# Token rows first and unmodulated transposes in the prologue of a hybrid diffusion step

## The reference, cut to what matters

```python
mod = silu(c) @ ada_w + ada_b            # 6 rows of 1024 per group: sh1, sc1, g1, sh2, sc2, g2
h   = rms_norm(x, norm_mix_pre) * (1.0 + sc1) + sh1
proj = h @ w_in                          # 1024 x 3072: xl, yl, q, k, v, g
# then: gated linear recurrence, retention, w_out, router, 16 SwiGLU experts
```

## Time and profile before

| what | value |
|---|---|
| profiled execution, its own time | 1585.94 us |
| its span | 1583.7 us |
| PE busy | 1395.2 us (88%) |
| DVE busy | 681.2 us (43%) |
| ACT busy | 269.6 us (17%) |
| POOL busy | 126.9 us (8%) |
| HBM read | 464.59 MB, 302 GB/s over the span |
| first projection matmul | 62.33 us from the span's start |

### The profile page before, as it was taken

How to read it: one execution, slowest core, us unless ns; L and a number is a source line. 1 busy time by engine, 2 the same in 40 slices (tenths; PEclk the granted TensorE clock), 3 DMA queues, 4 the chain that set the end, 5 groups by cost and what they waited for, 6 DMA issues and landing times.

```text
span 1583.7 us, 26100 instructions
## 1 busy us (share of the span) xinstructions
PE 1395.2 (88%) x11009; PEld 616.5 (39%) x11009; DVE 681.2 (43%) x1219; ACT 269.6 (17%) x448; POOL 126.9 (8%) x81
## 2 busy tenths in 40 slices
PE   5799889777963899999999999999999999999990
PEld 1587666544850222233333333333333333333330
DVE  1535654341454435245343444443534435335343
ACT  2324444220330011101101111011110111101102
POOL 0422331120000000000000000000000000000000
PEclk9999999887976899999999999999999999999995
DMA  9421120357043999999999999999999999999973
GB/s 361 139 80 54 53 67 30 117 181 263 28 186 133 377 395 396 398 415 396 411 398 397 412 388 408 398 395 406 396 397 406 391 392 395 399 414 394 412 296 141
DMA packets 124272, 479.79 MB, mean 303 GB/s; under 512 B 11534, under 2 KB 13834, under 8 KB 107788
## 3 DMA queue, kind: packets, MB, share of 16 engines
q1 hardware_dynamic: 113796, 453.55, 72.9%
q0 software_dynamic: 3072, 10.49, 2.8%
q10 hardware_dynamic: 7304, 14.23, 2.5%
HBM read 464.59 MB, written 13.64 MB: 302 GB/s over the span
## 4 chain that ended last, share of the span: by engine, by line
PE 64%; DMA 22%; DVE 9%; ACT 3%; issue 2%; ACTq 0%; POOL 0%; SPq 0%; POOLq 0%; DVEq 0%
PE bank L1031 18%; DMA arena<-in_exp_up 13%; PE bank L1048 12%; PE bank L1036 9%; PE bank L1053 6%; DMA raw<-in_exp_up 5%; PE bank L359 3%; PE bank L360 3%; PE bank L361 3%; DMA raw<-in_ada_w 2%; PE bank L742 1%; DVE arena L1231 1%; PE bank L792 1%; PE bank L874 1%; PE bank L851 1%
## 5 line engine op out<-in xcount | busy, mean ns | idle before, releaser
L1031 PE MATMUL bank<-raw,xs_t 128*32 128x512 f32 x1056 | 257.3, 604 | 45.4 <-DMA raw<-in_exp_up 16.9
L1033 PE MATMUL bank<-raw,xs_t 128*32 128x512 f32 x1040 | 250.0, 602 | 0.0
L1031 PE MATMUL bank<-arena,xs_t 128*32 128x512 f32 x992 | 238.4, 596 | 6.2 <-DVE arena L1470 5.2
L1033 PE MATMUL bank<-arena,xs_t 128*32 128x512 f32 x1008 | 240.7, 599 | 0.0
L1467 DVE SCALAR_TENSOR_TENSOR arena<-bank,gate,arena 64x512 f32<-64x512 f32 x64 | 73.6, 1150 | 325.2 <-ACT arena L684 323.8
L1036 PE MATMUL bank<-raw,xs_t 128*16 128x512 f32 x1048 | 206.0, 603 | 0.0
L1036 PE MATMUL bank<-arena,xs_t 128*16 128x512 f32 x1000 | 198.0, 595 | 0.0
L1419 DVE STREAM_TRANSPOSE arena<-arena 32x256 f32<-32x256 f32 x372 | 161.8, 435 | 79.0 <-PE bank L1053 73.2
L684 ACT ACTIVATE arena<-bank 64x512 f32<-64x512 f32 x64 | 37.7, 588 | 831.1 <-PE bank L1036 830.3
L1031 PEld LDWEIGHTS bank<-raw,xs_t 128*32 128x32 f32 x1056 | 70.8, 111 | 207.7 <-issue 194.0
L1419 DVE STREAM_TRANSPOSE xs_t<-arena 32x256 f32<-32x256 f32 x204 | 88.8, 435 | 104.5 <-DMA arena<-xn_rows,slot_tok 101.5
(11 more groups left out here) (219 smaller groups left out, 1609.8 us busy)
## 6 DMA issues: line engine op xcount, KB each, us to landing
raw<-in_exp_gate SPq DMA_DIRECT2D x66, 1024.0 KB, 13.5
raw<-in_exp_up SPq DMA_DIRECT2D x65, 1024.0 KB, 14.5
arena<-in_exp_down SPq DMA_DIRECT2D x64, 1024.0 KB, 14.6
raw<-in_exp_down SPq DMA_DIRECT2D x64, 1024.0 KB, 12.6
arena<-in_exp_up SPq DMA_DIRECT2D x63, 1024.0 KB, 14.6
arena<-in_exp_gate SPq DMA_DIRECT2D x62, 1024.0 KB, 12.7
raw<-in_ada_w SPq DMA_DIRECT2D x24, 1024.0 KB, 9.1
raw<-in_w_in SPq DMA_DIRECT2D x12, 1024.0 KB, 5.9
```

What stands on the lines that cost most here:

```text
L1031: mm(psum[b][32 * i:32 * i + 32, :], lat[i], g[:, j, c], start=first, stop=final)
L1033: mm(psum[b][64 + 32 * i:96 + 32 * i, :], lat[i], u[:, j, c], start=first, stop=final)
```

## The change

- SP's queue issues the five loads of `x_in` ahead of all weights; ScalarE's queue no longer does. ScalarE's loads of the router weights and the rope tables come after the scaling of the token rows.
- ScalarE scales tiles 1 and 3, VectorE 0, 2 and 4.
- The second and third ada blocks change places (first half of the scale ahead of second half of the shift), and w0 lands ahead of a4.
- TensorE transposes the unmodulated rows between the first ada chunks; ScalarE (latent) and VectorE (context) bring them out into eight buffers `xT`. VectorE makes `hT_tmp` (now four buffers) from `xT` in SBUF. `hT_lo` is made by VectorE for k-tiles 0, 2, 4, 6, 7 and by GpSimd for 1, 3, 5.
- Chunk w0 goes k-tile by k-tile over all five output tiles, with the third ada block behind k-tile 0, the fourth ada block and the third's columns behind k-tile 1, and the fourth's columns behind k-tile 2. Then TensorE waits for k-tiles 4 to 7.

The core of the diff:

```diff
-ADA_FIRST = [0, 1, 2, 3]
+ADA_FIRST = [0, 2, 1, 3]
-LANDING = ([("a", i) for i in range(8)] + [("w", i) for i in range(12)] + ...
+LANDING = ([("a", i) for i in range(4)] + [("w", 0)] + [("a", i) for i in range(4, 8)] + [("w", i) for i in range(1, 12)] + ...
+    xT = [region(10240 + kt * TOK if kt < 4 else 2688 + (kt - 4) * TOK, TOK) for kt in range(KT)]
 # SP
+        for t in range(TILES):
+            sync.dma_start(x_in[:, t, :], x_lat[t * P:(t + 1) * P, :] if t < 4 else x_ctx).then_inc(x_ld[t], 16)
 # ScalarE
+            act.wait_ge(x_ld[t], 16)
...
+            nc.scalar.activation(junk0, x_in[:, t, :], ACT.Square, accum_out=...).then_inc(x_sq, 1)
+            if t == 2:
+                act.wait_ge(par_rd, 1)
+                nc.scalar.activation(sil, par[:, R_C:R_C + 16], ACT.Silu).then_inc(sil_rd, 1)
...
+        root(S_RSTD)
+        act.wait_ge(root_out, 1)
+        for t in (1, 3):
+            nc.scalar.mul(x_in[:, t, :], x_in[:, t, :], sm[:, S_RSTD + t:S_RSTD + t + 1]).then_inc(xn_act, 1)
         act.dma_start(rw[:, :, :], router_w.rearrange("(k p) n -> p k n", p=P)).then_inc(rw_in, 16)
         act.dma_start(rope_c, rope[0]).then_inc(rope_in, 16)
         act.dma_start(rope_s, rope[1]).then_inc(rope_in, 16)
+        for kt in range(KT):
+            xT_out(kt)
+            if kt == 5:
+                split_hi(act, 0)
+        for kt in range(4):
+            h_out(kt)
...
+        split_hi(act, 1)
+        for kt in range(4, KT):
+            h_out(kt)
+        split_hi(act, 2)
 # TensorE
+        pe.wait_ge(cond_rd, 1)
+        ada_block(0, 5)
+        pe.wait_ge(xn_rd, 3)
+        pe.wait_ge(xn_act, 2)
+        for kt in range(4):
+            turn_x(kt)
+        ada_half(1, 6, 0)
+        turn_x(4)
+        turn_x(5)
+        columns(0, 7, 128)
+        ada_half(1, 6, 1)
+        turn_x(6)
+        turn_x(7)
+        columns(1, 4, 128)
...
+            if n == 0:
+                for k in range(4):
+                    h_ready(pe, k)
+                    for u in range(TILES):
...
+                    if k == 0:
+                        pe.wait_ge(ada_row, 1)
+                        ada_block(2, 5)
+                    if k == 1:
+                        pe.wait_ge(ada_row, 2)
+                        ada_block(3, 6)
+                        pe.wait_ge(col_rd, 1)
+                        columns(2, 7, 128)
+                    if k == 2:
+                        pe.wait_ge(col_rd, 3)
+                        columns(3, 7, 128)
+                for kt in range(4, KT):
+                    h_ready(pe, kt)
+                continue
 # VectorE
+        row_copy(0, 5, rows[:, 0:512])
+        for kt in range(6):
+            xT_out(kt)
+        col_out(0, 7, 128)
         row_copy(1, 6, rows[:, 0:512])
+        xT_out(6)
+        xT_out(7)
         col_out(1, 4, 128)
+        aff_half(0)
+        h_out(0)
+        h_out(1)
+        split_lo(dve, "dve", 0)
+        h_lo_out(0)
+        h_out(2)
+        h_out(3)
+        h_lo_out(2)
+        row_copy(2, 5, rows[:, 0:512])
+        col_out(2, 7, 128)
         row_copy(3, 6, rows[:, 0:512])
+        col_out(3, 7, 128)
+        aff_half(1)
+        for kt in range(4, KT):
+            h_out(kt)
+            if kt >= 5:
+                if kt - 1 in (4, 6):
+                    h_lo_out(kt - 1)
+        split_lo(dve, "dve", 1)
+        h_lo_out(7)
+        split_lo(dve, "dve", 2)
 # GpSimd
+        split_lo(pool, "pool", 0)
+        h_lo_out(1)
+        h_lo_out(3)
+        split_lo(pool, "pool", 1)
+        h_lo_out(5)
+        split_lo(pool, "pool", 2)
```

More of the change, by code:

```diff
@@ L334, in expert_used, with h_ready @@
         eng.wait_ge(x_used, e * PER_E + (n - N_EXP + 1))
+    def h_ready(eng, kt):
+        if kt in (1, 3, 5):
+            eng.wait_ge(h_lop, kt // 2 + 1)
+        else:
+            eng.wait_ge(h_lo, {0: 1, 2: 2, 4: 3, 6: 4, 7: 5}[kt])
     def ret_sums(h):
@@ L453, in _, with xT_out, h_out @@
         root(S_RSTD)
[L454 to L455 removed]
+        act.wait_ge(root_out, 1)
+        for t in (1, 3):
+            nc.scalar.mul(x_in[:, t, :], x_in[:, t, :], sm[:, S_RSTD + t:S_RSTD + t + 1]).then_inc(xn_act, 1)
+        act.dma_start(rw[:, :, :], router_w.rearrange("(k p) n -> p k n", p=P)).then_inc(rw_in, 16)
+        act.dma_start(rope_c, rope[0]).then_inc(rope_in, 16)
+        act.dma_start(rope_s, rope[1]).then_inc(rope_in, 16)
+        def xT_out(kt):
+            act.wait_ge(xT_ps, kt + 1)
+            nc.scalar.copy(xT[kt][:, 0:LAT], psum[kt % 2][:, :]).then_inc(xe_lat, 1)
+        def h_out(kt):
+            act.wait_ge(h_tmp, kt + 1)
+            nc.scalar.copy(hT_hi[:, kt, :], hT_tmp[:, kt % 4, :]).then_inc(h_hi, 1)
+        for kt in range(KT):
[4 more added lines that the diff above has]
+            h_out(kt)
         act.wait_ge(lam_abs, 1)
         nc.scalar.activation(sm[:, S_EXP:S_EXP + 8], sm[:, S_ABS:S_ABS + 8], ACT.Exp, scale=-1.0).then_inc(lam_exp, 1)
[L459 to L461 removed]
+        split_hi(act, 1)
+        for kt in range(4, KT):
+            h_out(kt)
+        split_hi(act, 2)
         def yl_out(ct):
@@ L756, in columns, with turn_x @@
             last.then_inc(col_ps, 1)
[L759 to L773, removed]
+        def turn_x(kt):
             if kt >= 2:
-                pe.wait_ge(h_tmp, kt - 1)
+                pe.wait_ge(xe_lat, kt - 1)
+                pe.wait_ge(xe_ctx, kt - 1)
             for t in range(4):
@@ L820, in _ @@
             chunk_ready(pe, n)
-            pe.wait_ge(h_lo, 4 * (half + 1) if bi == 0 else KT)
             wh, wl = chunk_view(w_hi, n, 512), chunk_view(w_lo, n, 512)
+            if n == 0:
[3 more added lines that the diff above has]
+                        if k == 0:
+                            bank_free(0, u)
+                        if u < 4:
+                            last = three(psum[u][:, :], wh[:, k, u * P:(u + 1) * P], wl[:, k, u * P:(u + 1) * P],
+                                         hT_hi[:, k, 0:LAT], hT_lo[:, k, 0:LAT], k == 0, False)
+                        else:
+                            last = three(psum[4][:, :], hT_hi[:, k, LAT:], hT_lo[:, k, LAT:], wh[:, k, :], wl[:, k, :], k == 0, False)
+                    if k == 3:
+                        last.then_inc(w_used, 1)
+                    if k == 0:
+                        pe.wait_ge(ada_row, 1)
[11 more added lines that the diff above has]
+                continue
             for u in range(TILES):
@@ L1148, in _ @@
[L1148 to L1161, removed]
+        for t in (0, 2, 4):
+            ts(x_in[:, t, :], x_in[:, t, :], sm[:, S_RSTD + t:S_RSTD + t + 1], None, ALU.mult).then_inc(xn_rd, 1)
@@ new lines, in xT_out, with h_out @@
+        def xT_out(kt):
+            dve.wait_ge(xT_ps, kt + 1)
+            cp(xT[kt][:, LAT:], psum[2 + kt % 2][:, 0:P]).then_inc(xe_ctx, 1)
+        def h_out(kt):
+            if kt >= 4:
+                h_ready(dve, kt - 4)
+            else:
+                dve.wait_ge(xe_lat, kt + 1)
+                dve.wait_ge(xe_ctx, kt + 1)
+            ts(hT_tmp[:, kt % 4, 0:LAT], xT[kt][:, 0:LAT], aff[:, 0, 0, kt:kt + 1], modc[:, 0, kt:kt + 1], ALU.mult, ALU.add)
+            ts(hT_tmp[:, kt % 4, LAT:], xT[kt][:, LAT:], aff[:, 0, 1, kt:kt + 1],
+               modc[:, 1, kt:kt + 1], ALU.mult, ALU.add).then_inc(h_tmp, 1)
@@ new lines, in h_lo_out, with aff_half @@
+        def h_lo_out(kt):
+            dve.wait_ge(h_hi, kt + 1)
+            tt(hT_lo[:, kt, :], hT_tmp[:, kt % 4, :], hT_hi[:, kt, :], ALU.subtract).then_inc(h_lo, 1)
+        def aff_half(half):
+            k4 = slice(4 * half, 4 * half + 4)
+            dve.wait_ge(col_rd, 2 * half + 2)
+            for g in range(2):
+                step(stt(aff[:, 0, g, k4], modc[:, g, 8 + 4 * half:12 + 4 * half], 1.0, par[:, R_PRE + 4 * half:R_PRE + 4 * half + 4],
+                         ALU.add, ALU.mult))
@@ L1513, in _, with h_lo_out @@
         nc.gpsimd.memset(cond[:, :, :], 0.0).then_inc(cond_0, 1)
-        for n in range(WS):
-            split_lo(pool, "pool", n)
         nc.gpsimd.memset(gw[0], 0.0).then_inc(gw_0, 1)
+        def h_lo_out(kt):
+            pool.wait_ge(h_hi, kt + 1)
+            nc.gpsimd.tensor_tensor(hT_lo[:, kt, :], hT_tmp[:, kt % 4, :], hT_hi[:, kt, :], ALU.subtract).then_inc(h_lop, 1)
+        split_lo(pool, "pool", 0)
[4 more added lines that the diff above has]
+        split_lo(pool, "pool", 2)
         pool.wait_ge(col_ps, 4)
         nc.gpsimd.memset(gw[1], 0.0).then_inc(gw_0, 1)
-        for kt in range(KT):
-            pool.wait_ge(h_hi, kt + 1)
-            nc.gpsimd.tensor_tensor(hT_lo[:, kt, :], hT_tmp[:, kt % 2, :], hT_hi[:, kt, :], ALU.subtract).then_inc(h_lo, 1)
         for m in range(N_WOUT):
```

38 lines of the change are left out of this document (19 added, 19 removed).

## The result

The change made the kernel 1.0% faster, more than twice what I had forecast.

A forecast was written before the change was run, and what follows sets the result against it. Experts fill TensorE, busy 88%, untouched; the chain of waits in the first 66 us was asked. Its terms end w1 at 83.5 instead of 91.3, 7.8 us: 1585.94 - 7.8 = 1578.1, range 1573.3 to 1584.0.

The forecast's parts named there:

- Landings and token rows: Prologue loads and row scaling: a1 lands at 16.3 us, w0 at 26.2; rows are scaled by 16.9 and cost nothing.
- rival with the stuck queue: ScalarE stuck issuing rope loads until 23.2 us, time 1581.4; 20% together with one fall of the clock.
- TensorE to the end of the transposes: From 18.2 us, transposes, ada chunks and columns all at the low clock level, ending at 34.4.
- the clock never holds: TensorE stays at the low level to the last columns, costing 12.9 us; time 1591.0, slower; chance 5%.
- larger gain: VectorE ahead of w0 and w1: no blocking and `hT_tmp` at 0.6, 4.6 us more gained, time 1573.5; chance 10%.
- the blocking: GpSimd's subtraction holds up VectorE's SBUF operations, charged 1.54 us before the first matmul and again ahead of w1.
- VectorE to the first matmul: After the transposes, column step, `hT_tmp`, low split, GpSimd's 1.54 and `hT_lo`: TensorE starts w0 at 40.8 us.
- w0, k-tile by k-tile: TensorE from w0's start to the last columns: k-tile 0 5.2 us, the rest at the high level, together 17.7.
- The new wait: VectorE's work behind the last columns takes 9.7 us, to 68.2; TensorE idles 6.3 us behind k-tile 3.
- w1: Second projection chunk costs 13.5 + 1.8 us, its clock low after the idle time, ending at 83.5 instead of 91.3.
- The shift is carried: Everything behind w1 is written relative to TensorE, so the 7.8 us shift reaches the end unchanged.

The follow-up runs named there:

- filled front: Changed kernel with four extra matmuls on constants, results not used, ahead of the first ada block; 1570.28 us, 0.9899 to the kernel before.
- transposes in twos: Changed kernel with transposed k-tiles reordered: two, half an ada block, two, columns, half an ada block, four; 1571.31 us in one run.
- before, filled: Kernel before the change with TensorE's gaps between transposed k-tiles filled by matmuls whose results are not used; 1582.86 us, 0.9991 to the kernel before.
- x first: Kernel before the change with only the five x loads moved to the head of SP's queue; 1585.7 us, 0.9993 to the kernel before.
- tile order: Changed kernel with chunk w0 done tile by tile, all eight hT k-tiles and all modulation work ahead of it; 1567.23 us, 0.9867 to the kernel before.
- ada behind k-tile 0: Changed kernel with third and fourth ada blocks and both sets of columns right behind w0's first k-tile; 1566.39 us, 0.9861 to the kernel before.

## Why the prediction was wrong

I had the owners and the order of the waits right. The step that failed is the second: I priced TensorE's work up to the end of the transposes at the low level throughout. In the order of the prediction's steps:

1. **Landings and token rows: held.** Chunk a1 was used at 16.06 (said: 16.3), w0 rounded at 25.09 (said: 26.2), the extra table load is there at 9.22, 1.28 us. The rope loads took 0.60 and 0.80 us of ScalarE's queue, not 4.58: the rival with the stuck queue fell.
2. **TensorE to the end of the transposes: the step that failed.** I summed it all at the low level, 34.4; it was 28.39. The two stretches of after, TensorE alone, columns as above:

```profile
16.00:22.00 6.00, 5.94 (x27) 1.00 1.09 367
22.00:28.00 6.00, 6.00 (x53) 1.00 1.08 370
```

   Both show 6 us of unbroken work and a granted clock of 1.00, but the first holds 27 records and the second 53. The column reads 1.00 in the first too, where the durations are those of half speed; the durations, not the column, tell the level there. I took the low level from the kernel before, where ada work, columns and transposes ran slowly from 29 to 43 us, and did not bound the term from the other side, which the same operations later in the kernel offered. At the high level throughout the 16.2 us from 18.2 on are 8.1, so the bound would have been 26.3, and 28.39 lies inside. I looked at the clock only as a danger (the rival "the clock never holds"), not as a gain. Of my rivals the "larger gain" comes nearest in time, 1573.5, but by luck: it wanted no blocking, and the blocking is there (steps 3 and 5).
3. **VectorE to the first matmul: 4.75 instead of 6.4.** A k-tile of `hT_tmp` took 0.72, not 0.85, and GpSimd's price fell on GpSimd: its subtraction took 2.97 us (1544 ns mean in the earlier trace rows), since VectorE's split, begun at 30.45, was already under way at 31.37. VectorE's own `hT_lo` at 32.12 went ahead of it at its usual 0.81.
4. **w0, k-tile by k-tile: 19.0 instead of 17.7.** The clock fell in the gap of 4.75 us and stayed down for all of k-tile 0: 6.4 us for 15 matmuls (PEclk 0.53) where I had 5.2. How long it stays down is not the gap's length alone: behind 5.70 us in the filled front it was nine matmuls. From k-tile 1 on it ran high, as forecast: 12.7 us.
5. **The new wait: right, its size partly by luck.** 52.2 to 61.75 is 9.55 us, forecast 9.7; the idle time 5.9, forecast 6.3. The k-tiles (0.72 each) and the blocking (1.3) came out 0.8 us cheaper together, and handovers between the engines, which I had put at nothing, took about as much. VectorE's line in that place, timeline of after:

```profile
53.65 0.54 DVE L1212 TENSOR_SCALAR arena<-arena,aff,modc 128x512 f32<-128x512 f32 x1
...
55.27 1.83 DVE L1212 TENSOR_SCALAR arena<-arena,aff,modc 128x512 f32<-128x512 f32 x1
55.28 1.54 POOL L1610 TENSOR_TENSOR act_lo<-arena,act_hi 128x640 fp32r<-128x640 f32 x1 [6.08 <-ACT act_hi L476]
```

   The same scaling takes 0.54 us alone and 1.83 where GpSimd's subtraction, 1.54, starts within 0.01 us of it: 1.3 us more. The Trainium skill (SBUF — State Buffer, "Who interferes with whom") says of such a pair that whoever issues first has the shared ports for the whole instruction and the other is fully blocked. The trace agrees that one of the two waits, here VectorE, by 1.3 of the 1.54 us; which was issued first, starts 0.01 us apart don't tell. In step 3, where VectorE's operation is a subtraction with two inputs in SBUF, GpSimd pays.
6. **w1: 15.9 instead of 15.3**, low again behind the gap (PEclk 0.85).

The terms by size, steps 2 to 6: -6.0, -1.65, +1.3, -0.15, +0.6; together -5.9, and w1 ends at 77.6 where I had 83.5. Carried to the end, that makes 1572.2. The median is 1569.3. The terms are not independent: of 2.2 us taken from the transposes in the filled front, 1.2 reached the first projection matmul.

7. **The shift is carried: right to within 3 us.** Median less gates is 1461.2 for after and 1464.4 for before (1460.9 and 1461.7 the second time). These last 3 us are not settled. The interval of the gain, 13.6 to 18.7, includes the 13.7 us found up to gates, and the stretch behind gates differs by 5 us between two executions of the kernel before.

Open as well is what decides when the clock rises. The run of transposes is not it (transposes in twos), nor is any transpose needed. Timeline of TensorE in the kernel before and then in "before, filled", whose order up to 40 us is the same:

```profile
36.41 1.87 PE L754 MATMUL bank<-const,rows 128*128 128x2 f32 x8
```

```profile
32.48 3.52 PE L742 MATMUL bank<-raw,cond 128*32 128x512 f32 x16
35.92 1.05 PE L754 MATMUL bank<-const,rows 128*128 128x2 f32 x8
```

The same set of columns takes 1.87 us in one and 1.05 in the other, ahead of any transpose and any filling; "x first" has 1.05 there too. The second trace of before has 1.87, although its ada work starts within 0.05 us of that of "before, filled" (32.53). So the kind, order and timing of the work seen here don't settle the level, and the earlier trace rows, from which I took it, show one of two outcomes.

By the experiments, then, the gain up to gates comes so: in tile order the new order of the front gives 18.6 us (121.78 to 103.20), of which 8.4 hang on the early landing of w0 and 10.2 on the rest, the clock's earlier rise included; x loaded first, alone, gives nothing, and a clock raised ahead of w0 gives 2.7 in the kernel before. The k-tile order then takes 4.9 away.

## What to carry to other kernels

Bound every duration that depends on the clock from both levels, also where the row at hand shows only one: another execution of the same order can show the other. Before work is made finer to start early, look for what the late half will wait for: here moving small pieces of modulation work into a gap and behind k-tile 0 and an earlier split won 8.6 us up to gates, where the order by k-tiles had cost 4.9. A weight that lands late also holds whatever stands behind its split in that engine's queue: the wait of 11.41 us fell on the columns of another block.

## What was not expected of the hardware

- Behind a gap of 4.75 us TensorE was at its low level for the next 6.4 us (15 matmuls at 0.43 us instead of 0.23); with the gap filled by unused matmuls the clock stayed at 1.00. It also fell with no gap over 1 us, at 46 us of "ada behind k-tile 0" (granted clock 0.50), behind ada work and columns.
- With TensorE at its high level from 16.4 us on, transposes and columns ended at 26.22 instead of 28.39, but the first projection matmul came only 1.2 us earlier, and no difference shows in the time.
- A queue that held a 256 KB load for 4.58 us when the x loads stood ahead of it took it in 0.60 us without them. "x first" shows that it is not the moment: issued at 8.62 us there, 8.71 in before, the load took 0.60 us too.
